# Score masks and position biases by rounded products in a two-block layer kernel

## The reference

```python
# sliding window (8 heads of 64) and block attention (8 heads of 64): a bias by distance
logits = einsum(q, k) * HEAD_DIM ** -0.5 + bias_tab[rel_bucket(qpos - kpos)]
logits = where(mask, logits, NEG)
# forgetting attention (8 heads): cumulated log gates c, causal
logits = einsum(q, k) * HEAD_DIM ** -0.5 + c[q] - c[k];  where(k <= q, logits, NEG)
# second block, differential attention (4 heads, 2 maps each): mask by chunks of 64
s = einsum(q, k) * DIFF_HEAD_DIM ** -0.5;  softmax(where(k_chunk <= q_chunk, s, -inf))
```

## Time and profile before

| | us |
|---|---|
| median of 3 runs | 1839.09 |
| lowest, highest | 1838.37, 1848.33 |
| the profiled execution | 1835.87 |
| its span | 1834.1 |
| PE busy in the span | 1652.2 (90%) |
| DVE busy | 736.9 (40%) |
| ACT busy | 486.5 (27%) |
| POOL busy | 146.6 (8%) |
| DMA queue of the weights | 519.62 MB, 73.4% of 16 engines' span |

### The profile page before, as it was taken

The page is one execution under the profiler, slowest core; times in us unless marked ns, Lnnn a source line. Parts: engine busy times, 40 slices in busy tenths (PEclk is TensorE's granted clock), DMA queues, the critical chain, the costliest instruction groups (busy, mean ns, idle before and its releaser), DMA issues.

```text
span 1834.1 us, 22968 instructions
## 1 busy us (share of the span) xinstructions
PE 1652.2 (90%) x9892; PEld 1049.3 (57%) x9892; DVE 736.9 (40%) x1260; ACT 486.5 (27%) x816; POOL 146.6 (8%) x180
## 2 busy tenths in 40 slices
PE   6999999989999999898999888888898888888885
PEld 5998888878999988797433232323232222323221
DVE  5667754677886466664321121212111111112122
ACT  4344454445554344352210010101000000001001
POOL 1200000320552003000100000000000000000000
PEclk8999999999999999999999999999999999999998
DMA  7563422544665452553999999999999999999995
GB/s 194 177 195 111 122 74 88 160 144 134 186 184 184 160 167 70 172 185 127 352 422 425 422 424 422 425 424 424 424 423 425 423 425 423 425 424 424 424 424 235
DMA packets 209322, 525.97 MB, mean 287 GB/s; under 512 B 18009, under 2 KB 134670, under 8 KB 176446
## 3 DMA queue, kind: packets, MB, share of 16 engines
q1 hardware_dynamic: 206830, 519.62, 73.4%
q0 software_dynamic: 2384, 4.82, 1.1%
HBM read 523.31 MB, written 1.07 MB: 286 GB/s over the span
## 4 chain that ended last, share of the span: by engine, by line
PE 43%; DMA 30%; DVE 2%; ACT 1%; issue 0%; POOL 0%; SPq 0%; ACTq 0%; DVEq 0%
PE bank L591 41%; DMA slot_ring<-in_w_down 8%; DMA slot_h_hi<-in_w_down 5%; DMA slot_high<-in_w_down 5%; DMA slot_memn<-in_w_down 3%; DMA slot_last<-in_w_down 3%; DMA slot_late<-in_w_down 3%; DMA slot_high<-in_w_gu 1%; DMA slot_late<-in_w_gu 1%; DMA slot_ring<-in_w_gu 1%; PE bank L1067 1%; DVE rot_tmp L2145 0%; DVE x_sb L1778 0%; ACT L1385 0%; POOL bias_r L1370 0%
## 5 line engine op out<-in xcount | busy, mean ns | idle before, releaser
L591 PE MATMUL bank<-h_hi_r,high_r 128*128 128x256 f32 x1000 | 286.5, 287 | 9.1 <-DVE slot_ring_r L1770 9.1
L1770 DVE TENSOR_TENSOR slot_ring_r<-slot_ring,high_r 128x1024 fp32r<-128x1024 f32 x200 | 245.8, 1272 | 96.7 <-ACT high_r L1385 96.6
L591 PE MATMUL bank<-h_lo_r,high_r 128*128 128x256 f32 x1000 | 284.4, 284 | 0.0
L591 PE MATMUL bank<-h_hi_r,slot_ring_r 128*128 128x256 f32 x952 | 270.9, 285 | 0.0
L1774 DVE TENSOR_SCALAR ga<-bank 128x512 f32<-128x512 f32 x32 | 22.1, 692 | 591.5 <-PE bank L591 591.5
L1385 ACT ACTIVATE high_r<-slot_ring 128x1024 fp32r<-128x1024 f32 x200 | 199.9, 1053 | 64.9 <-PE bank L591 54.6
L591 PEld LDWEIGHTS bank<-h_hi_r,high_r 128*128 128x128 f32 x1000 | 192.7, 193 | 9.9 <-DVE slot_ring_r L1770 9.8
L591 PEld LDWEIGHTS bank<-h_lo_r,high_r 128*128 128x128 f32 x1000 | 192.6, 193 | 0.1
L1385 ACT ACTIVATE th_e<-ga 128x512 f32<-128x512 f32 x32 | 20.2, 630 | 626.4 <-DVE ga L1774 626.4
L591 PEld LDWEIGHTS bank<-h_hi_r,slot_ring_r 128*128 128x128 f32 x952 | 183.2, 192 | 0.0
L591 PE MATMUL bank<-slot_ring,xg 128*64 128x512 f32 x600 | 142.1, 600 | 12.2 <-DMA slot_ring<-in_w_gu 12.2
(11 more groups left out here) (398 smaller groups left out, 2916.9 us busy)
## 6 DMA issues: line engine op xcount, KB each, us to landing
slot_ring<-in_w_gu SPq DMA_DIRECT2D x75, 1024.0 KB, 22.1
slot_high<-in_w_gu SPq DMA_DIRECT2D x64, 1024.0 KB, 22.1
slot_ring<-in_w_down SPq DMA_DIRECT2D x47, 1024.0 KB, 21.4
slot_late<-in_w_gu SPq DMA_DIRECT2D x37, 1024.0 KB, 21.9
slot_ring<-in_w_in SPq DMA_DIRECT2D x36, 1024.0 KB, 4.9
slot_memx<-in_w_gu SPq DMA_DIRECT2D x27, 1024.0 KB, 22.1
slot_memt<-in_w_gu SPq DMA_DIRECT2D x27, 1024.0 KB, 22.3
slot_ring<-in_w_up SPq DMA_DIRECT2D x44, 512.0 KB, 4.6
```

What stands on the lines that cost most here:

```text
L591: return e.matmul(o, lhs, rhs, start=start, stop=stop, skip_group_check=True)
L1770: return e.tensor_tensor(o, i, j, op)
```

## The change

Masks and biases are added by products in the rounded type. `flip` and the two masks are rounded in place, `ident` into a tile of its own (it goes on serving transposes in float32), by ScalarE behind the rounding of the first weight tile. A mask is rounded and multiplied once. A bias row is split: ScalarE writes the rounded value, VectorE the rest, both go to `diag_dram`, and each `toep` tile holds both parts (128x512 in place of 128x256), with four buffers in place of eight; `flip` is multiplied with the value and with the rest. Some constants are reordered and padded by five columns.

```diff
-        toep_in = [load_sem(f"toep{i}") for i in range(8)]
+        toep_in = [load_sem(f"toep{i}") for i in range(4)]
...
-        diag_dram = nc.dram_tensor("diag_dram", (BIAS_H, TOEP), F32).ap()
+        diag_dram = nc.dram_tensor("diag_dram", (2, BIAS_H, TOEP), F32R).ap()
...
+        flip_r = rounded("flip", const_cols["flip"][0], P)
+        masks_r = rounded("masks", const_cols["causal"][0], 2 * S)
...
+        ident_r = small("ident_r", P, dt=F32R)
...
-        toep = [at(f"toep{i}", AR + i * S, S) for i in range(8)]
+        toep = [rounded(f"toep{i}", AR + i * 2 * S, 2 * S) for i in range(4)]
...
                     if kind == "fox":
                         matmul(b[:, c], fox_pair(fox_l, n)[:, qs], fox_pair(fox_rt, n)[:, ks], False, False)
-                        m = matmul(b[:, c], ident, C("causal")[:, cs], False, True)
+                        q.wait_ge(*act["masks"])
+                        m = matmul(b[:, c], ident_r, masks_r[:, 0:S][:, cs], False, True)
                     else:
-                        m = matmul(b[:, c], C("flip"), toep[(2 * n + (kind == "moba")) % 8][:, cs], False, True)
+                        bias = tiles(toep[(2 * n + (kind == "moba")) % 4], 2)
+                        q.wait_ge(*act["masks"])
+                        matmul(b[:, c], flip_r, bias[:, 0, cs], False, False)
+                        m = matmul(b[:, c], flip_r, bias[:, 1, cs], False, True)
...
-                        last = matmul(bank(name)[:, c], ident, C("chunk1")[:, cs], False, True)
+                        last = matmul(bank(name)[:, c], ident_r, masks_r[:, S:2 * S][:, cs], False, True)
...
-                e.dma_start(diag_dram[i * SWA_H:(i + 1) * SWA_H, :], diag_sb[i]).then_inc(*diag_out.step("diag"))
+                for j, part in enumerate((diag_s[i].hi, diag_s[i].lo)):
+                    e.dma_start(diag_dram[j, i * SWA_H:(i + 1) * SWA_H, :], part).then_inc(*diag_out.step("diag"))
...
-                if n >= 8:
-                    q.wait_ge(*pe["scores", kind, n // 2 - 4])
-                src = bass.AP(diag_dram.tensor, head * TOEP, [[1, P], [1, S]])
-                e.dma_start(toep[n % 8], src).then_inc(*toep_in[n % 8].step("toep", n))
+                if n >= 4:
+                    q.wait_ge(*pe["scores", kind, n // 2 - 2])
+                src = bass.AP(diag_dram.tensor, head * TOEP, [[1, P], [BIAS_H * TOEP, 2], [1, S]])
+                e.dma_start(tiles(toep[n % 4], 2), src).then_inc(*toep_in[n % 4].step("toep", n))
...
             ahead(("ub", 0), 0)
+
+            for i in range(2):
+                evac(("diag hi", i), diag_s[i].hi, bank(f"diag{i}")[0:SWA_H, 0:TOEP], "diag")
+            af(masks_r, const_sb[:, const_cols["causal"][0]:const_cols["causal"][0] + 2 * S], ACT.Copy).then_inc(*act.step())
+            af(flip_r, C("flip"), ACT.Copy).then_inc(*act.step())
+            af(ident_r, ident, ACT.Copy).then_inc(*act.step("masks"))
...
             for i in range(2):
-                q.wait_ge(*pe["diag"])
-                e.tensor_copy(diag_sb[i], bank(f"diag{i}")[0:(SWA_H, MOBA_H)[i], 0:TOEP]).then_inc(*dve.step("diag", i))
+                q.wait_ge(*act["diag hi", i])
+                tt(diag_s[i].lo, bank(f"diag{i}")[0:SWA_H, 0:TOEP], diag_s[i].hi, ALU.subtract).then_inc(*dve.step("diag", i))
```

More of the change, by code:

```diff
@@ L80, in shape_constants @@
             freq[p, 0] = base[(p % HD) % half]
-    parts["freq"] = freq
     parts["iota2"] = np.tile(np.arange(CAP), (P, 2))
-    parts["part"] = i[:, None]
-    parts["slot"] = i[:, None] % CAP
     parts["owners"] = np.concatenate([(i[:, None] // 64 == c) & (i[:, None] % NE == np.arange(NE)) for c in range(2)], axis=1)
@@ L93, in shape_constants @@
     parts["invc"] = inv
+    parts["freq"] = freq
+    parts["part"] = i[:, None]
+    parts["slot"] = i[:, None] % CAP
+    parts["pad"] = np.zeros((P, 5))
     m = np.arange(TOEP)
@@ L348, in hybrid_moe_program @@
         fox_l, fox_rt = area("fox_l", 2 * S), area("fox_rt", 2 * S)
-        diag_sb = [at(f"diag{i}", SCORE + i * TOEP, TOEP)[0:n, :] for i, n in enumerate((SWA_H, MOBA_H))]
+        diag_s = [Split(*(rounded(f"diag_{part}{i}", SCORE + (2 * i + j) * TOEP, TOEP)[0:SWA_H, :]
+                          for j, part in enumerate(("hi", "lo")))) for i in range(2)]
         PAD = CONV_W - 1
@@ L352, in hybrid_moe_program @@
         conv = tiles(area("conv", BT * S), BT)
-        th_conv = [at(f"th_conv{i}", PROB + i * S, S) for i in range(2)]
-        toep = [at(f"toep{i}", AR + i * S, S) for i in range(8)]
+        th_conv = [at(f"th_conv{i}", PROB + TOEP + i * S, S) for i in range(2)]
+        toep = [rounded(f"toep{i}", AR + i * 2 * S, 2 * S) for i in range(4)]
         conv_sq = glu[:, :, 0:S]
@@ L675, in tensor_program @@
                 *pe.step("diag"))
-            banks.give("diag0", (dve, ("diag", 0)))
-            banks.give("diag1", (dve, ("diag", 1)))
+            banks.give("diag0", (act, ("diag hi", 0)), (dve, ("diag", 0)))
+            banks.give("diag1", (act, ("diag hi", 1)), (dve, ("diag", 1)))
             for c in range(BT):
@@ L725, in scores @@
                     q.wait_ge(*dve["ka"])
-                    q.wait_ge(*toep_in[2 * n % 8]["toep", 2 * n])
+                    q.wait_ge(*toep_in[2 * n % 4]["toep", 2 * n])
                 elif kind == "moba":
@@ L730, in scores @@
                     q.wait_ge(*dve["kd", 1])
-                    q.wait_ge(*toep_in[(2 * n + 1) % 8]["toep", 2 * n + 1])
+                    q.wait_ge(*toep_in[(2 * n + 1) % 4]["toep", 2 * n + 1])
                 else:
```

## The result

The changed kernel takes 1856.64 us (median of 6 runs, 1853.99 to 1859.7), the kernel before 1838.73 us beside it (6 runs). The ratio is 1.0097, with a 95% interval of 1.0075 to 1.0118: slower by 1%, where 1822 us and faster were forecast. The profiled execution took 1854.14 us with a span of 1852.4 us, 18.3 us more than before. The mean granted clock of its span is 0.959.

A forecast was written before the change was run, and what follows sets the result against it. TensorE was taken to bound the attention rounds, VectorE close behind. Savings of 13.4 us in the rounds and 3.4 us in the differential attention summed to 16.8 us, giving 1822 us, range 1815 to 1831.

The forecast's parts named there:

- The price of a product: TensorE's scores: 256 and 128 columns take 0.63 and 0.42 us in fp32, 0.12 and 0.11 us rounded.
- The new order has as many steps in as out, so these cancel: TensorE's scores: changing between fp32 and rounded products gives 0.10 us less one way, 0.09 more the other, netting nothing.
- the 16.0: Eight attention rounds: 16.0 us of TensorE time saved at 2.0 us each, 13.4 kept after a wait for VectorE.
- the 6.6: Differential attention: eight mask additions save 6.6 us at 0.82 each, of which 3.4 us were taken as kept.
- Rival 3: Scores: each new product shows its 0.11 us weight load; a round saves 0.9 us, giving 1829 us; chance 0.08.
- The clock: Scores: falls of the granted clock cost 1.5 us each; their unknown number puts +6 to -6 us into the range.
- I leave four in the sum and take 0 to 8: Eight rounds: four clock falls of some 3 us stay in the forecast, 0 to 8 are allowed in its range.
- VectorE as the next bound: TensorE waits for VectorE 2.6 us in the third round and some 3 us ahead of the last differential attention transposes.
- Rival 2: Clock falls in all eight rounds and once or twice in differential attention give back 9 us: 1831 us; chance 0.15.
- Rival 4: Scores: a rounded product beside fp32 ones takes the fp32 time, a bias costs 1.05 us more: 1856 us; chance 0.02.
- ScalarE's five extra instructions: Start of the kernel: roundings and copies cost ScalarE 2 to 3 us, delaying TensorE by zero, at most 1.5 us.

The follow-up runs named there:

- e3: The changed kernel with the biases in fp32 again, masks rounded in both blocks: 1841.47 us.
- e8: The changed kernel with gate projection pieces between kinds of scores, value projections spread, and each score's low-row products ahead of its rounded ones: 1819.96 us, ratio 0.9892.
- e12: The kernel before, masks and biases in fp32, with the order and cutting of e8: 1828.18 us, ratio 0.9939.
- e10: The changed kernel with 128 rows in place of 64 for the differential attention's query-key products (output not the reference's): 1845.02 us, one run.
- e11: The kernel before, all fp32, with 72 rows in place of 128 for the differential attention's mask products: 1853.97 us, one run.
- e4: The changed kernel with each round's gate projection cut in four pieces among the scores and value projections spread between differential maps: 1830.24 us, ratio 0.9943.
- e13: e8 with fewer passages between heights: two kinds' 64-row products together, 2-row products behind 64-row ones, both maps of a head together: 1817.57 us, ratio 0.9883.
- e2: The changed kernel with all masks in fp32 again, only the biases rounded: 1855.75 us.
- e1: The kernel before with only the eight masks of the differential attention rounded: 1848.84 us, one run.
- e9: The changed kernel with each score's low-row products ahead of its rounded ones, without any cutting: 1830.3 us, one run.

## Why the prediction was wrong

- **The price of a product: the step that failed first.** "0.63 / 0.42 us" was read off fp32 products that stand between products of another height, and put down to the format. At full height they cost 0.43 and 0.22; the rest are passages, which the rounded products inherit. "The new order has as many steps in as out, so these cancel" compared passages between two full-height kinds and overlooked those between heights, which stay on both sides. At full height a mask would save 0.65 - 0.23 = 0.42 us; between low products it saves 0.48, not 0.82, and a bias 0.24, not 0.59. A round saves 2 x 0.24 + 0.39 = 0.9 us at most (0.39 is what the stretch of scores lost in e3, 7.13 to 6.73 us) and not 2.0; e8 against e12 shows 0.77 (rounds of 19.95 and 20.72 us). That leaves 6 to 7 us of the 16.0 and 3.8 of the 6.6.
- **Rival 3** had nearly these sizes (0.9 us a round, 0.15 and 0.60), but its mechanism fell: a second rounded product behind a first costs 0.44 - 0.31 = 0.13 us (a bias pair less a mask, 256 columns), so not each product shows its weight load. The rule of the Trainium skill ("TensorE: Matmul & The Clock Gate", Part 3) that a load overlaps only with products of other row groups would show the load at every change from one full-height product to the next, as their row groups are the same. The trace disagrees: in the full-height map of e10 nothing is left for it (0.88 us), and the dear passage is the one from 64 to 128 rows, where the groups differ in part.
- **The clock: the step that decided the sign.** "I leave four in the sum and take 0 to 8" counted falls of 3.4 us. All eight rounds fell, six of them for 6.8 us and one for 10.2, and the differential attention for 20.5 us at a stretch. A fall that starts within the scores stretches them, in the first round to 152.40 - 143.95 = 8.45 us, against 7.2 before with dearer products; that it prolongs itself so is a guess. The row that spoke for it was in the text ("the full-height products between them shrink"), and it was taken to speak for more falls as much as for fewer. What changed heights do to the clock is shown in the differential attention (e11), and only there.
- **The sum with measured terms.** By the earlier trace rows a fall of 3.4 us costs 1.5 us, 0.43 for each microsecond that is low. Rounds: -8 x 0.77 + 41.0 x 0.43 = +11.5, measured +10.5. Differential attention: -3.8 + 20.5 x 0.43 = +5.0, measured +5.0. The sum for the rounds is 1 us too high. The cross attention adds 3.4 us, with 10.2 us more low; none of its instructions was changed, and the prediction had nothing there.
- **VectorE as the next bound** (2.6 us in the third round, 3 us behind the differential scores) never came, since TensorE didn't get ahead. In e4, where it did, the wait was there, up to 1.5 us in six rounds, and in e13 also 4.7 us in the differential attention. The mechanism was right, its condition wasn't met.
- **Rival 2** (more falls, 1831) had the mechanism and not the size. **Rival 4** reached the measured time, 1856, by a cause that isn't there: two rounded bias products of 256 columns cost 0.44 us and not twice 0.63.
- **What held.** ScalarE's five extra instructions took 27.94 - 26.28 = 1.7 us at the start, a little under the 2 to 3 forecast, and moved no score later; it came 0.9 us earlier. TensorE waited for no bias tile. What was lost ahead of the experts arrived at the end in full, their own time changed by 0.8 us.

```profile
26.28 0.83 ACT L1395 ACTIVATE diag_hi_r<-bank 8x384 fp32r<-8x384 f32 x2
27.94 3.88 ACT L1395 ACTIVATE high_r<-slot_ring 128x1024 fp32r<-128x1024 f32 x4
```

**Open.** In the first block it is shown that the biases bring the low clock (e2, e3) and that cutting the scores takes it away (e4), but changed heights were tried in the second block alone; that the same cause acts in the first is inferred. One number speaks against a simple form of it: e2, with fp32 masks, was low for 61.4 us in the rounds and the changed kernel, with rounded ones on top, for 54.6; between two single executions that can be chance. The longer low time of the cross attention goes with the differential attention's scores: 17 to 18 us in the changed kernel, e1, e3 and e11, 7 in the kernel before and e2. But e9, whose scores had no fall, has 18 us too, so the way isn't shown.

## What to carry to other kernels

Price a product by a row in which its neighbours have the height that they will have after the change, and look for a row of the same kind in a stream: what differs between the two is a passage, and it stays. Making full-height products cheaper between products of few rows cost more by the clock here than it saved, though TensorE was never idle; in such a case mix full-height work into such a stretch and group products by height, as e4 and e8 did. Here the change by itself lost 18 us, and the same change with grouped and spread scores is 20 us faster than the kernel before.

## What the runs showed of the hardware

- A passage between products of 64 (or 2) and 128 rows costs TensorE 0.17 to 0.20 us at 2.4 GHz, whether the 128-row product is rounded (e9, e10 against the changed kernel) or fp32 (the kernel before). One between fp32 and rounded products of full height costs next to nothing (e10: 0.88 us a map, the sum of the stream prices).
- In the scores of the changed kernel the granted clock fell to 1.2 GHz while TensorE was busy in every window. With the same count, format and distances of products it was low for 0 us of the stretch with 128-row masks and for 27.3 us with 72-row ones (e11, one execution).
- Each microsecond at 1.2 GHz cost 0.43 us of the time in a round (1.5 us for 3.4) and in the differential attention (8.8 us for 20.5); in the output and feed-forward stretch 6.8 us more of it cost nothing that shows.
